# Two half projections in split single-pass products, and a router that reads rows before their norm, in a three-layer decoder kernel

## The reference, cut to what matters

```
h = layer_norm(alpha * x + mixer(x), g, b)
g_prob  = softmax(h @ w_rg + b_rg)            # 4 groups, the best one is taken
e_logit = h @ w_re + b_re                     # 32 experts, the best 2 of that group
gate    = softmax(top 2 of e_logit in the group) * g_prob[group]
y       = sum over the two experts of gate * (silu(h @ w1) * (h @ w3)) @ w2
x       = layer_norm(alpha * h + y, ...)
```

## Time and profile before

| | us |
|---|---|
| median of 3 runs | 1523.52 |
| the profiled execution, its own time | 1520.87 |
| its span (first to last instruction) | 1519.1 |
| PE busy | 1471.6 (97%) |
| DVE busy | 552.5 (36%) |
| ACT busy | 466.8 (31%) |
| POOL busy | 153.8 (10%) |
| DMA, mean of the span | 331 GB/s |

### The profile page before, as it was taken

One profiled execution on the slowest core, in us unless ns is written; L12 is line 12 of the kernel. 1 busy time (PEld: TensorE's weight loads), 2 busy tenths in 40 slices (PEclk: granted clock), 3 DMA queues, 4 the chain that ended last, 5 costly groups with the idle time before them and its releaser, 6 DMA issues.

```text
span 1519.1 us, 19195 instructions
## 1 busy us (share of the span) xinstructions
PE 1471.6 (97%) x7726; PEld 879.3 (58%) x7726; DVE 552.5 (36%) x1151; ACT 466.8 (31%) x819; POOL 153.8 (10%) x126
## 2 busy tenths in 40 slices
PE   8989999999999999999999999999999999999998
PEld 7755454544544444977544545445444786788886
DVE  6645111111111114037321111211111487688965
ACT  4541111111111113456111111111111561577654
POOL 0211000000000002953100000000000610001200
PEclk9999999999999999999999999999999999999999
DMA  8655999999999999835899999999999846464410
GB/s 300 249 222 221 373 424 427 428 428 427 428 426 428 428 423 398 301 145 238 330 411 426 428 426 428 427 428 428 428 426 409 322 177 220 168 214 174 170 53 28
DMA packets 76228, 502.68 MB, mean 331 GB/s; under 512 B 4720, under 2 KB 6000, under 8 KB 49136
## 3 DMA queue, kind: packets, MB, share of 16 engines
q1 hardware_dynamic: 75280, 495.18, 79.9%
q0 software_dynamic: 864, 6.29, 1.0%
HBM read 500.40 MB, written 1.05 MB: 330 GB/s over the span
## 4 chain that ended last, share of the span: by engine, by line
PE 87%; DMA 5%; DVE 4%; ACT 2%; issue 1%; SPq 1%; POOL 0%; DVEq 0%; ACTq 0%
PE bank L1057 26%; PE bank L1090 14%; PE bank L916 9%; PE bank L1003 7%; PE bank L1374 6%; DMA ring<-in_w_up 4%; PE bank L1402 4%; PE bank L863 4%; PE bank L1017 3%; PE bank L1376 3%; PE bank L882 1%; PE bank L950 1%; PE bank L798 1%; SPq L606 1%; PE bank L1072 1%
## 5 line engine op out<-in xcount | busy, mean ns | idle before, releaser
L1057 PE MATMUL bank<-ring,arena 128*64 128x512 f32 x1280 | 284.2, 599 | 12.0 <-issue 6.8
L1057 PEld LDWEIGHTS bank<-ring,arena 128*64 128x64 f32 x1280 | 94.4, 138 | 196.8 <-issue 192.7
L1057 PE MATMUL bank<-arena 128*64 128x512 f32 x576 | 168.3, 592 | 3.5 <-issue 3.5
L2037 DVE TENSOR_TENSOR arena<-arena,bank 128x512 f32<-128x512 f32 x32 | 22.0, 688 | 383.0 <-PE bank L1057 383.0
L1090 PE MATMUL bank<-ring,arena 128*64 128x512 f32 x640 | 141.7, 595 | 2.4 <-ACT arena L1556 2.4
L1374 PE MATMUL bank<-x_split,w_high 128*128 128x512 f32 (+1 forms) x408 | 139.1, 392 | 0.2 <-DVE x_split L1845 0.2
L1003 PEld LDWEIGHTS bank<-SEL,x_by_row 128*128 128x128 f32 x1024 | 116.7, 192 | 25.8 <-issue 24.3
L1003 PE MATMUL bank<-SEL,x_by_row 128*128 128x128 f32 x1024 | 122.8, 278 | 0.0
L2051 DVE SCALAR_TENSOR_TENSOR y_low<-bank,ST,y_high 128x512 fp32r<-128x512 f32 x64 | 48.1, 751 | 202.4 <-ACT y_high L1560 202.4
L1560 ACT ACTIVATE y_high<-bank,ST 128x512 fp32r<-128x512 f32 x64 | 44.0, 687 | 245.6 <-PE bank L1090 245.6
L1057 PEld LDWEIGHTS bank<-arena 128*64 128x64 f32 x576 | 55.3, 137 | 110.7 <-issue 110.7
(11 more groups left out here) (352 smaller groups left out, 2247.3 us busy)
## 6 DMA issues: line engine op xcount, KB each, us to landing
ring<-in_w_gate SPq DMA_DIRECT2D x32, 2048.0 KB, 27.2
ring<-in_w_up SPq DMA_DIRECT2D x32, 2048.0 KB, 22.5
ring<-in_w_down SPq DMA_DIRECT2D x32, 2048.0 KB, 24.3
arena<-in_w_gate SPq DMA_DIRECT2D x18, 2048.0 KB, 24.2
arena<-in_w_up SPq DMA_DIRECT2D x18, 2048.0 KB, 24.5
arena<-in_w_down SPq DMA_DIRECT2D x18, 2048.0 KB, 25.9
ring<-in_ffn_up SPq DMA_DIRECT2D x12, 2048.0 KB, 8.8
ring<-in_w_in SPq DMA_DIRECT2D x8, 2048.0 KB, 13.6
```

The source lines that it names most:

```text
L1057: last = nc.tensor.matmul(bank[4 + m][64 * e:64 * e + 64, :], XG[:, c, 64 * e:64 * e + 64], w[e][:, c, :], start=(c == 0), stop=(c == C - 1))
```

## The change

Three things change.

1. The projection of the differential heads (layer 0) and of retention (layer 2) is split. ACT makes eight high rows of weights, DVE eight low ones (the low ones lie over the weights themselves), and the transposed features are split as they leave their banks. The 16 float32 products become 48 single-instruction ones.
2. The router reads rows before their norm. With u the row before the norm, m its mean and r its inverse deviation, `layer_norm(u) @ W + b` equals `r * (u @ (g * W - mean over features of g * W)) + (b + shift @ W)`. The folded weights are made once per layer: for layer 0 on PE with `norm_columns` and `route_sums` in the midst of layer 0's attention, for layer 1 on DVE during its QKV projection (`sum_routes`), with one product on PE.
3. The order around the choice. Tile 0 is transposed and its logits are taken inside the projection of tile 1; `choose` is issued per tile; tile 1's norm stands ahead of its own choice. ACT scales tile 0, and POOL applies gain and shift (`finish_x`); ACT makes `XP`. Both tiles' residual products stand behind tile 1's norm. The `keep_clock` calls of the router are gone.

```diff
-            def rows_of_x(l):
-                pool.wait_ge(x_ready, 4 * l + 2)
-                for t in range(T):
-                    nc.gpsimd.tensor_copy(XP[:, t, :, :], ...)
+            def finish_x(l):
+                pool.wait_ge(ln_loaded, 16 * (2 * l + 1))
+                pool.wait_ge(x_scaled, l + 1)
+                link(nc.gpsimd.tensor_tensor(X[:, 0, :], X[:, 0, :], LNR[:, 0, :], ALU.mult))
+                nc.gpsimd.tensor_tensor(X[:, 0, :], X[:, 0, :], LNR[:, 1, :], ALU.add).then_inc(x_ready, 1)
...
+            def norm_columns():
+                pe.wait_ge(ln_loaded, 16)
+                for a in range(2):
+                    for c in range(C):
+                        last = nc.tensor.matmul(bank[0][:, a * C + c:a * C + c + 1], LNR[:, a, c * P:(c + 1) * P], ident[:, 0:1],
+                                                start=True, stop=True)
+                last.then_inc(rank_done, 1)
+            def route_sums():
+                pe.wait_ge(route_weights, 1)
+                for a in range(2):
+                    for c in range(C):
+                        last = nc.tensor.matmul(bank[0][:, (a + 1) * ROUTE:(a + 2) * ROUTE],
+                                                gain_shift[:, a, c:c + 1].broadcast_to([P, P]), WR[:, 0, c, :],
+                                                start=(c == 0), stop=(c == C - 1))
+                last.then_inc(rank_done, 1)
+            def route(l, name, g0):
+                logits(l, name, 1, [0])
+                x_transposes(name, g0, 1, [1])
+                logits(l, name, 1, [1])
+                pe.wait_ge(r_one, T * l + 1)
...
+                pe.wait_ge(x_ready, 4 * l + 2)
+                keep_residual(0)
+                keep_residual(1)
+                pe.wait_ge(r_one, T * l + 2)
+                nc.tensor.matmul(bank[4][:, 320:320 + EXPERTS], earlier, ELOG[:, 1, :], start=False, stop=True)\
+                    .then_inc(rank_done, 1)
...
             d_values(2)
+            norm_columns()
             d_transposes(3)
...
             k_transposes([2, 3])
+            route_sums()
             transposed("kb")
...
-            transposed("ao")
-            project_out(G_EO, I_EO, range(A_HEADS), first=A_HEADS, final=A_HEADS - 1)
-            transposes_by_token("ln0", X, x_ready, 0, [0])
-            pe.wait_ge(pj_free[1], G_EO + 1)
-            moe_layer(0, "ln0")
+            def beside_even(t, n, c):
+                if (t, n, c) == (1, 0, 1):
+                    x_transposes("ln0", G_EO, 0)
+                if (t, n, c) == (1, 1, 0):
+                    pe.wait_ge(route_weights, 2)
+                    logits(0, "ln0", 0)
+                if (t, n, c) == (1, 1, 2):
+                    x_transposes("ln0", G_EO, 1, [0])
+            project_differential(beside_even)
+            route(0, "ln0", G_EO)
+            moe_layer(0)
...
+            def mixed_norm(l, name):        # ACT
+                norm_root(0)
+                evac_whole_token(name, 0)
+                act.wait_ge(x_prepared, 2 * l + 1)
+                nc.scalar.activation(X[:, 0, :], X[:, 0, :], ACT.Identity, scale=rs_l[:, 0:1], bias=neg_mean)\
+                    .then_inc(x_scaled, 1)
+                evac_whole_token(name, 1)
+                norm_root(1)
...
+            def mixed_norm(l, g0, name):    # DVE
+                for t in range(T):
+                    for n in range(2):
+                        if (t, n) == (1, 1):
+                            choose(l, 0)
+                        add_half(g0, t, n, ALPHA)
...
+                dve.wait_ge(tr_done, sum(TR[name]))
+                dve.wait_ge(x_ready, 4 * l + 1)
+                v.scalar_tensor_tensor(X[:, 1, :], X[:, 1, :], mv[:, 1, 0:1], LNR[:, 0, :], ALU.subtract, ALU.mult)
+                norm_scale(1)
+                choose(l, 1)
...
+            def choose(l, t):
+                dve.wait_ge(logits_done, T * l + t + 1)
+                link(v.scalar_tensor_tensor(LOG[:, t, :], bank[4 + t][:, 0:ROUTE], rs_l[:, t:t + 1], route_bias(l),
+                                            ALU.mult, ALU.add))
+                link(v.tensor_reduce(m0[:, t:t + 1], LOG[:, t, 0:GROUPS], AX, ALU.max))
+                first_of(LOG[:, t, 0:GROUPS], GROUPS, m0, i0)
+                link(v.tensor_scalar(mask, io_g, i0[:, t:t + 1], NEG, ALU.not_equal, ALU.mult))
+                link(v.tensor_tensor_reduce(...))
+                first_of(ONE2[:, t, :], EXPERTS, m1, i1)
...
```

More of the change, by code:

```diff
@@ L249, in bass_two_blocks @@
         gmn, gsum, gw = stat(T), stat(T), stat(T)
-        m1, m2, i1, i2, p2, g1, g2 = (stat(T) for _ in range(7))
+        m0, i0, m1, m2, i1, i2, p2, g1, g2 = (stat(T) for _ in range(9))
+        neg_mean, gain_shift = stat(1), stat(2, C)
         rtop, rtop2 = stat(1), stat(1)
@@ L712, in _ @@
             last.then_inc(ao_ready, 1)
-            rows_of_x(0)
+            finish_x(0)
             next_norm_rows(0, 1)
@@ L850, in recurrence_tile, with project_out @@
                 return LX[:, c, t * P:(t + 1) * P]
-            def retention_tile(c, t):
-                return YRT[:, c - LRU_T, t * P:(t + 1) * P]
-            def project_out(g0, i, rows=range(C), tile=mixed_tile, beside=None, first=0, final=C - 1):
+            def project_out(g0, i, rows=range(C), tile=mixed_tile, beside=None, first=0, final=C - 1, between=None):
                 for t in range(T):
@@ L864, in project_out @@
                                                     slot(i[n], C, 512)[:, c, :], start=(c == first), stop=(c == final))
+                            if between is not None and c != final:
+                                between(t, n, c)
                         if rows[-1] == final:
@@ L868, in project_out, with project_out_split @@
                             beside()
-            def project_out_split(beside):
+            def project_out_split(beside, between):
                 for t in range(T):
@@ L886, in project_out_split, with project_retention, project_differential @@
                             beside()
+            def project_retention(beside):
+                for t in range(T):
+                    tok = slice(t * P, (t + 1) * P)
+                    for n in range(2):
+                        for h in range(RET_HEADS):
+                            k = RET_HEADS * n + h
+                            if t == 0:
+                                pe.wait_ge(o_lo, RET_LOW_FROM + k + 1)
+                            for m, (a, b) in enumerate(((RHI, RET_HIGH), (RHI, RET_LOW), (RLO, RET_HIGH))):
+                                last = nc.tensor.matmul(bank[(G_OUT2 + n) % 2 * 2 + t][:, :], a[:, h, tok], b[k],
+                                                        start=False, stop=(h == RET_HEADS - 1 and m == 2))
+                        last.then_inc(pj_done, 1)
+                        if (t, n) == (T - 1, 0):
+                            beside()
+            def project_differential(between):
+                for t in range(T):
+                    tok = slice(t * P, (t + 1) * P)
+                    for n in range(2):
+                        first = (t, n) == (0, 0)
+                        kinds = ((DHI, EVEN_HIGH), (DHI, EVEN_LOW), (DLO, EVEN_HIGH))
+                        order = [(m, c) for m in range(3) for c in range(A_HEADS)] if first else \
+                            [(m, c) for c in range(A_HEADS) for m in range(3)]
+                        for m, c in order:
+                            a, b = kinds[m]
+                            k = A_HEADS * n + c
+                            if first and m == 0 and c % 2 == 0:
+                                pe.wait_ge(m_hi, c // 2 + 1)
+                            if first and m == 2 and c % 2 == 0:
+                                pe.wait_ge((tr_act, tr_dve)[c // 2], sum(TR["ao"]) // 2)
+                            if t == 0 and m == 1:
+                                pe.wait_ge(o_lo, k + 1)
+                            last = nc.tensor.matmul(bank[(G_EO + n) % 2 * 2 + t][:, :], a[:, c, tok], b[k],
+                                                    start=False, stop=(c == A_HEADS - 1 and m == 2))
+                            if m == 2 and c != A_HEADS - 1:
+                                between(t, n, c)
+                        last.then_inc(pj_done, 1)
             def project_t(g, i):
@@ L997, in x_spread, with gather @@
                 return X[:, t, :].rearrange("p (q c) -> p c q", c=C)[:, c, :]
-            def gather(s, x_rows):
+            def gather(s, x_rows, ready=None):
                 for c in range(C):
+                    if ready is not None and c % 4 == 0:
+                        pe.wait_ge(*ready[c // 4])
                     for t in range(T):
@@ new lines, in x_transposes @@
+            def x_transposes(name, g0, t, halves=range(2)):
+                for h in halves:
+                    k = TR[name][0] + 2 * t + h
+                    pe.wait_ge(pj_free[t], g0 + h + 1)
```

(21 more changed lines are left out.)

276 lines of the change are left out of this document (169 added, 107 removed).

## The result

| | before | after |
|---|---|---|
| median of 14 runs each | 1521.99 us | 1526.76 us |
| lowest and highest | 1518.97, 1524.50 | 1521.23, 1533.72 |
| ratio, 95% interval | | 1.0032, 1.0020 to 1.0045 |
| profiled execution, its span | 1520.87, 1519.1 | 1525.64, 1523.8 |
| mean granted clock of its span | 0.998 | 0.989 |

The change costs 4.9 us (0.0032 x 1522), with an interval of 3.0 to 6.8. I had forecast no change that can be told, -0.5. The time lies inside the range, near its upper end, and close to rival C (1528.1). All the later figures against before are worked out in the same way, ratio less one times 1522.

A forecast was written before the change was run, and what follows sets the result against it. Transfers bound the experts of layers 0 and 1, started by each gather; PE bounds layer 2. Layer 0 +1.1, layer 1 -1.75, layer 2 -1.6 and clock +1.7 sum to -0.55 us: 1523.0, range 1516.5 to 1528.5.

The forecast's parts named there:

- rival C: Routers of layers 0 and 1: clock falls through residual, ranks and gather make it slower, four falls give 1528.1; chance 0.19.
- The bound: Experts of layers 0 and 1: transfers set their length, so a microsecond before a gather moves their end by a microsecond.
- Split products, -3.1 for each half: Half projections, layers 0 and 2: 16 float32 products fall from 13.97 to 10.9 us when split, 3.1 us saved.
- Layer 0's way to the gather with the lock, -7.1 + 2.3: Layer 0, projection to gather: gather 7.1 us earlier, 2.3 given back because tile 0's choice on DVE waits for POOL.
- Layer 1 the same, -3.5 + 1.5: Layer 1, projection to gather: gather 3.5 us earlier, 1.5 given back because tile 0's choice waits for POOL.
- My sign for a right forecast, the gather at 735.6: Layer 1's gather near 735.6 in the profile would show the forecast right.
- layer 0's +1.1: Layer 0's total: -7.1 to the gather, +2.3 from POOL and DVE, +5.9 from folded weights, +1.1 us.
- The lock: Router: DVE's choice for tile 0 waits for POOL's `finish_x` instruction; 2.3 us lost in layer 0, bounds 0 and 4.8.
- The folded weights, +5.9: Layer 0's attention: small products for `norm_columns` and `route_sums` take 7.8 us on PE, 5.9 lost; bounds 2.0 and 7.8.
- rival B: Layer 0's folding is half as dear because one-column products cost less; -6.15 us, 1517.4; chance 0.13.
- Layer 2, -1.6: Layer 2's split projection, after waits for casts and subtractions, gains 1.6 us; bounds 1.0 and 2.3.
- The clock, +1.7: Routers without `keep_clock`: one price of a clock fall, 1.7 us, for layers 0 and 1 together; bounds 0 and 6.8.

The follow-up runs named there:

- s_again: The kernel before plus the split products in both half projections alone, measured once more; 0.9971, -4.4 us against before.
- kg_lock: The changed kernel with layer 0's folding wholly on DVE and 256-column `keep_clock` products in the router's waits, `finish_x` still on POOL; 0.9963, -5.6 us against before.
- v_dve: The changed kernel with `finish_x`'s two instructions moved from POOL to DVE, ahead of tile 0's choice; 1.0020, +3.0 us against before.
- p_extra: The kernel before with the 64 small folding instructions added at the change's two places in layer 0's attention, results unused; 1.0075, +11.4 us against before.
- s_split: The kernel before plus the split products in both half projections alone, first measurement; 0.9968, -4.9 us against before.
- k2_clock: The changed kernel with `keep_clock` products of 256 columns put into PE's waits in both routers; 1.0009, +1.4 us against before, -3.5 against the changed kernel.
- g_fold: The changed kernel with layer 0's folding moved to DVE under the first half projection; 1.0000, -4.9 us against the changed kernel.
- k_clock: The changed kernel with `keep_clock` products of two instructions, 0.88 us each, put into PE's waits in both routers; 1.0022, +3.3 us against before.
- p_wide: The kernel before with eight float32 products of 512 columns added at two places in layer 0's attention, results unused; 1.0051, +7.8 us against before.
- g_again: The changed kernel with layer 0's folding and `finish_x` on DVE and 256-column `keep_clock` products, second measurement; 0.9953, -7.2 us against before.

## Why the prediction was wrong, step by step

- **The bound** held: the gather's delay arrives at the end of the experts, to 0.5 us in the changed kernel and to 1.3 in all traces.
- **Split products, -3.1 for each half:** right. Alone they are worth 4.9 and 4.4 us in two measurements; by my working 3.1 + 0.5 - 0.3 in layer 0 and 1.6 in layer 2, 4.9. From the first half projection to the gather `s_again` is 3.36 us shorter than before, for the 3.3.
- **Layer 0's way to the gather with the lock, -7.1 + 2.3:** right to a tenth where the clock stays up. `kg_lock` has 41.57 us from the first half projection to the gather, before had 46.46: -4.9, forecast -4.8. The parts agree too: the choice with the locked step takes 5.2 us for the 5.4 that I placed, the last half's addition and the norm 4.4 for 4.5, the residual 3.70 for 3.6, ranks and selection 1.1 for 1.3. In the changed kernel it is -3.2.
- **Layer 1 the same, -3.5 + 1.5:** `kg_lock` has 36.53 for before's 38.60, -2.1, forecast -2.0. In the changed kernel it is +0.6. My sign for a right forecast, the gather at 735.6, was wrong by itself: it left out layer 0's +1.1, with which it is 736.7. Measured was 745.24.
- **The lock** was right in kind and near in size: one step of 2.08 in layer 0, 2.46 in layer 1, which ends with POOL's. It is 1.85 longer than the same step without POOL, for the 2.3 that I gave back. In layer 0 the locked step is a `tensor_scalar`. The Trainium skill (SBUF — State Buffer, Who interferes with whom) counts that form among those that can be locked, and this trace agrees, with 2.08 us instead of the 0.23 that the same line takes in tile 1's choice.
- **The folded weights, +5.9:** over-priced by themselves, 7.0 us of products instead of 7.8, and 4.75 on the chain where nothing falls (35.91 us in `v_dve` from the end of the input projection to the first scores, 31.17 before). The low bound, 2.0, and rival B are out: the 32 one-column instructions take 3.47, 0.108 each. But their own time isn't all they cost, as `p_extra` shows.
- **Layer 2, -1.6:** -0.9, under my lower bound of 1.0. The wait for the second subtraction came as forecast (start of the second half 16.38 after that of the first, instead of 15.60); what I had not priced is the handover behind it. Before the change the first product of the feed-forward part started 0.57 us ahead of the end of the projection's last product; now it starts 0.16 us ahead, so 0.4 us of overlap is gone. And the second half took 12.99 us instead of 15.06, 2.1 less where 3.1 - 0.6 was counted. The same 29.21 stands in the trace of `s_split`.
- **The clock, +1.7:** this is the step that failed. "I take one such price for both layers" stood for one fall of 1.7 us; the runs showed one in each router, at 1.66 us in layer 0 and 2.8 in layer 1 of the profiled execution, 4.5 in all. `k2_clock`, whose residual is at full clock, is 3.5 faster by its runs. The bounds of 0 and 6.8 held it. My reason for one price was the stretch at 481, in which PE was a third busy and the clock did not fall; that was one case, and I gave rival C, whose mechanism this is, 0.19. That the total came near C's is partly luck: C had 6.8 in the routers, they cost 4.5, and the rest came from falls and waits that neither C nor the sum had.
- **What was missing altogether** are falls outside the routers. The changed kernel's trace has one at 73 to 77 (1.5 us, at PE's waits for the first softmaxes) and one in layer 1's attention (1.3). The clocks of its runs, 0.986 to 0.992 where before's runs have 0.993 to 0.998, say that it mostly has some.

Put together, with the trace's figures: 4.75 - 4.8 - 2.0 + 0.25 - 0.9 + 4.5 = +1.8. So with all of its terms right the sum would still have been 3 us short. Falls outside the routers 1.5 + 1.3, a wait for "issue" at layer 1's start 1.3 (below), a later start 1.8, the feed-forward's faster pace -2.1 and the experts -0.6 make another 3.2; 5.0 by this account, 4.8 in the table. By runs it looks simpler: of the 9.8 us that separate the changed kernel from its split halves alone, moving the folding off PE returns 4.9, filling PE's waits 3.5, moving POOL's two instructions 1.8, which sums to 10.2, measured each by itself on the changed kernel. But the agreement is partly chance. `g_fold` and `k2_clock` are also two of the three changed versions without the wait of 1.3 us at layer 1's start (last section). If that belongs to the kernel, as it seems, the folding is worth about 3.6 and the filled waits about 2.2 (estimates, 4.9 and 3.5 less 1.3), and some 2 of the 9.8 us stay without a name; and the 1.8 isn't clear of noise.

The Trainium skill (TensorE: Matmul & The Clock Gate, Part 1) would, by its rule on idle gaps, have set the clock's term to 0, because no wait was long enough. The measurement decides against it here: a residual of 5.26 and 6.40 us that goes back to 3.70 once the waits, the longest of them 2.3 and 1.6 us, are filled.

## What to carry to other kernels

Products that keep the clock up are part of a schedule: whoever shortens or reorders the work around PE's waits must put them back, sized by the trace to the wait and not beyond it. Work that is tiny in columns is not tiny on PE's chain, costs about 0.11 us an instruction here, and can lower the clock for what follows; an engine that idles (here DVE under a projection of 14 us) is its place. And a change of two parts should be measured as two: the half of it that was simple arithmetic held all of the gain, and the other half lost 9.8 us until its three prices were found; without them it is worth perhaps 2 us more.

## What the runs showed that was not expected

- **PE can be busy without a gap and lose its clock.** In `p_extra` the 8 us with the 32 one-column instructions in them, PE counted busy 8.00 of 8, stand at clock 0.86, and the stretches behind, with the 32 of 36 columns and the attention, at 0.71 and 0.79. In `v_dve` and the changed kernel the same 64 small instructions passed without a fall. So they don't always bring one: of the six traces with these products at these places four have the clock under 1.00 in the stretch from 78 to 94, and of the eight without any of them none has. What decides between the four and the two was not tried.
- **The clock falls at the same wait in one execution and not in another.** The first transfer of the input is there for PE at 5.12 us before and at 5.35 after, the second in time before and only at 8.16 after, with a wait of 0.84 us, where nothing was changed ahead of it; and PE's waits in the attention then come at another moment. In seven of the sixteen traces the clock is under 1.00 from 70 to 78. Of the fourteen in which nothing was moved into PE's wait there, the four whose input projection ends latest, after 55.4 us, all have that fall, and one of the other ten has it. So the moment may be what decides; nothing here varies it alone. `s_split` and `s_again` are the same kernel: the one falls there and takes 32.77 us from the end of the input projection to the first scores, the other doesn't and takes 31.15.
- **A wait that seems to belong to the program's layout.** Between layer 0's experts and layer 1's first product PE waits for nothing that the profile shows, from the timeline of the changed kernel:

```profile
603.15 1.06 PE L802 MATMUL bank<-KT,X 128*128 128x128 f32 x8 [1.61 <-issue]
```

  The stretch from the end of layer 0's experts to layer 1's second chunk is 22.8 to 22.9 us in twelve of the sixteen traces, and 21.5 in the kernel before, `k_clock`, `k2_clock` and `g_fold`. Executions of one kernel agree (`s_split` 22.81, `s_again` 22.80). No edit was made there; `p_extra` and `p_wide` differ from the kernel before only by products in layer 0's attention, and have it. The place lies behind a jump of PE over the code of further rounds (`pe.If(more > 0)`), and the transfers of the profile's instruction queue (q8) split the traces in the same way: in the twelve one starts 11.5 us after the experts' end, in the four at 9.0, 9.1, 14.7 and 14.8. That fits 1.3 us that go with where the instructions lie, and doesn't show it; no run moved the instructions alone.
- **The feed-forward part has two paces,** 205.2 to 205.6 us and 206.9 to 207.3 for the same products, again with one of each for `s_split` and `s_again`. A difference of 2 us between two traces is nothing there.
- The fastest version is `g_again`, -7.2 and -5.8 in its two measurements; the plain `s_split`, at -4.9 and -4.4, has most of that with none of the router's machinery.
